# Three products of split weights as two, evictions in two halves, and output projections begun beside the last attention heads

## The reference

```python
def swiglu(h, w1, w3, w2):
    return (jax.nn.silu(h @ w1) * (h @ w3)) @ w2

def retention_layer(x, g, w_in, w_mem_kv, w_out, mem_n):
    h = rmsnorm_2(x, g)
    q, k, v, gate_r, mq, gate_m = split_cols(h @ w_in, [...])
    q = rotary(q...); k = rotary(k...) * (RET_DK ** -0.5)
    o = retention(q, k, v)
    o = o * lax.rsqrt(jnp.mean(o * o, axis=-1, keepdims=True) + EPS)
    o_ret = o * jax.nn.silu(gate_r)
    o_mem = memory_branch(mq, gate_m, mem_n, w_mem_kv)
    return x + jnp.concatenate([o_ret, o_mem], axis=-1) @ w_out

def dilated_layer(x, g, w_in, w_mem_kv, w_out, mem_n, kv):
    parts = split_cols(rmsnorm_2(x, g) @ w_in, ...)
    outs, lses = [], []
    for gi, (window, dil) in enumerate(DIL_CONFIG):          # three groups, 16 heads
        o, lse = dilated_group(q, kv[2 * gi], kv[2 * gi + 1], dil, window // dil)
    alpha = jax.nn.softmax(jnp.stack(lses, axis=0), axis=0)
    o = jnp.sum(alpha[..., None] * jnp.stack(outs, axis=0), axis=0)
    o_dil = o * jax.nn.silu(gate_d)
    return x + jnp.concatenate([o_dil, o_mem], axis=-1) @ w_out
```

## Time and profile before

| | us |
|---|---|
| median of 3 runs (lowest, highest) | 4314.84 (4308.7, 4323.8) |
| profiled execution, its own time | 4317.47 |
| its span, first to last instruction | 4315.7 |
| PE busy | 4001.4 (93%) |
| ACT, DVE, POOL busy | 1566.1, 1525.2, 1355.2 |
| mean granted clock of PE | 0.967 of full |

### The profile page before, as it was taken

How to read it: one execution, slowest core, us unless ns; L and a number is a source line. 1 busy time by engine, 2 the same in 40 slices (tenths; PEclk the granted TensorE clock), 3 DMA queues, 4 the chain that set the end, 5 groups by cost and what they waited for, 6 DMA issues and landing times.

```text
span 4315.7 us, 95444 instructions
## 1 busy us (share of the span) xinstructions
PE 4001.4 (93%) x42564; PEld 3762.1 (87%) x42564; DVE 1525.2 (35%) x2011; ACT 1566.1 (36%) x1954; POOL 1355.2 (31%) x632
## 2 busy tenths in 40 slices
PE   8999999899888999999989999898999999999978
PEld 6876778788877899999989899788899999999978
DVE  2142116566555433332342333333222222222232
ACT  3342226421213443443434334344333333333333
POOL 2321122000003344444433344343333333333333
PEclk9999999899998999999989999899999999999989
DMA  9887663000004455555535444344545444455434
GB/s 320 280 294 261 222 238 119 26 4 4 4 10 148 154 186 182 182 186 183 182 124 164 149 153 162 126 155 148 174 151 164 159 152 146 152 162 161 150 124 132
DMA packets 183175, 668.39 MB, mean 155 GB/s; under 512 B 20432, under 2 KB 20432, under 8 KB 182384
## 3 DMA queue, kind: packets, MB, share of 16 engines
q1 hardware_dynamic: 176544, 642.07, 45.2%
q10 hardware_dynamic: 4944, 16.03, 1.1%
q0 software_dynamic: 1280, 4.20, 0.2%
HBM read 653.82 MB, written 8.39 MB: 153 GB/s over the span
## 4 chain that ended last, share of the span: by engine, by line
PE 84%; DVE 6%; ACT 3%; issue 3%; DMA 2%; POOL 1%; POOLq 0%; ACTq 0%; DVEq 0%; SPq 0%
PE ps L921 66%; PE ps L882 2%; PE ps L1138 2%; PE ps L1162 2%; PE ps L1152 1%; ACT wh L1389 1%; PE ps L1074 1%; DVE wl L1858 1%; PE ps L1377 1%; PE ps L1361 1%; DVE tm L1861 1%; ACT xw L1389 1%; DVE cols L2336 1%; PE ps L1263 1%; PE ps L861 1%
## 5 line engine op out<-in xcount | busy, mean ns | idle before, releaser
L921 PE MATMUL ps<-halves,wh 128*128 128x256 f32 (+1 forms) x13632 | 2620.2, 294 | 77.9 <-DVE halves L1858 19.7
L921 PEld LDWEIGHTS ps<-halves,wh 128*128 128x128 f32 x13632 | 2184.1, 195 | 147.1 <-issue 84.8
L921 PE MATMUL ps<-halves,wl 128*128 128x256 f32 (+1 forms) x6816 | 1983.3, 291 | 0.0
L2410 POOL TENSOR_TENSOR wl<-raw,wh 128x1024 fp32r<-128x1024 f32 x508 | 1235.4, 2433 | 2066.6 <-ACT wh L1389 2066.5
L1389 ACT ACTIVATE wh<-raw 128x1024 fp32r<-128x1024 f32 x1016 | 1072.1, 1057 | 1531.2 <-PE ps L921 1174.7
L1858 DVE TENSOR_TENSOR wl<-raw,wh 128x1024 fp32r<-128x1024 f32 x508 | 688.6, 1356 | 2037.4 <-ACT wh L1389 2037.4
L921 PEld LDWEIGHTS ps<-halves,wl 128*128 128x128 f32 x6816 | 1327.5, 195 | 13.2
L921 PE MATMUL ps<-wh,halves 128*128 128x256 f32 x2688 | 498.6, 285 | 0.0
L921 PEld LDWEIGHTS ps<-wh,halves 128*128 128x128 f32 x2688 | 423.5, 192 | 10.3 <-issue 9.1
L921 PE MATMUL ps<-wl,halves 128*128 128x256 f32 x1344 | 380.7, 283 | 0.0
L921 PEld LDWEIGHTS ps<-wl,halves 128*128 128x128 f32 x1344 | 258.4, 192 | 0.4
(11 more groups left out here) (243 smaller groups left out, 2505.6 us busy)
## 6 DMA issues: line engine op xcount, KB each, us to landing
raw<-in_ffn SPq DMA_DIRECT2D x264, 512.0 KB, 4.0
raw<-in_ada SPq DMA_DIRECT2D x192, 512.0 KB, 4.5
raw<-in_w_kv SPq DMA_DIRECT2D x192, 512.0 KB, 3.3
raw<-in_w_in_b SPq DMA_DIRECT2D x160, 512.0 KB, 3.9
raw<-in_w_in_a SPq DMA_DIRECT2D x128, 512.0 KB, 3.6
raw<-in_mem SPq DMA_DIRECT2D x64, 512.0 KB, 5.4
raw<-in_w_out_a SPq DMA_DIRECT2D x48, 512.0 KB, 4.1
raw<-in_w_out_b SPq DMA_DIRECT2D x48, 512.0 KB, 4.1
```

The costliest lines, as they stand in the source:

```text
L921: p = self.e.matmul(o, x, y, start=bi not in begun, stop=final and kc == 3 and m == 2, skip_group_check=True)
L2410: return self.e.tensor_tensor(out, a, b, op)
```

## The change

- `products` has two new kinds, "WB" and "WA". Of the three products of a slice and part, two become one with 512 columns: the high half of the weights meets high and low halves of the activations side by side (or the high half of the activations both halves of the weights). The 256-column product low by high is added into the first 256 columns. The two sums of high and low parts, in columns 0 to 255 and 256 to 511 of a bank, are added when they are taken out. So a job fills two banks of the four.
- Every such job is emptied in two operations: ACT copies the low columns, DVE adds the high ones (`low`, `high`, `finish_on`, `glu_gate`, `swiglu`, `ev_x` with four operations of DVE in place of two). The first five jobs' kind "both", `w_q`, `w_r`, `w_gd`, the first four jobs of `w_out`, and the first four of each output projection stay as they were.
- The rotation comes one tile later (`then_rotate`).
- Output projections: four jobs are begun with five of their six tiles beside the last heads (`EARLY`), and the tiles of the stream are ordered so.
- `pipeline_tight` puts 2, 3, 2, 4, 3 tiles between head steps in place of 2 each (`weave`).
- `wh` and `wl` become one buffer `whl`; the ring `w2` has ten places in place of eleven.

```diff
-    add("w_out_a", range(8), range(6))
+    def begun(name):
+        add(name, range(4), EARLY)
+        add(name, range(4), (3,))
+        add(name, range(4, 8), EARLY + (3,))
...
+def weave(g, steps, counts):
+    for n in itertools.cycle(counts):
+        rest(limited(g, n))
+        if next(steps, "end") == "end":
+            break
+    rest(g)
...
-                run_all((part(made[:7]), 2), (before, 1))
+                weave(part(made[:7]), before, (2, 3, 2, 4, 3))
...
+    def halved(self, kind, acts):
+        return [(i, 0, "WB", 128 * i, acts, 0) if kind == "B" else (i, 0, "WA", 0, acts, i) for i in range(2)]
...
-                if kind == "B":
+                if kind[0] == "W":
+                    o = self.G(job.banks[bi]).rearrange("p (a n) -> p a n", a=2)
+                    if kind == "WB":
+                        wh, wl = hi[:, kc, c0:c0 + 128], lo[:, kc, c0:c0 + 128]
+                        pairs = [(o[:, 0], wl, ah), (o, wh, self.hl[acts][:, :, k, :])]
+                    else:
+                        r = slice(128 * tb, 128 * tb + 128)
+                        both = self.A("whl")[:, :, t.n % NW, 256 * kc:256 * kc + 256]
+                        pairs = [(o[:, 0], al[:, r], hi[:, kc, :]), (o, ah[:, r], both)]
...
+    def then_rotate(self, g):
+        for _ in g:
+            if self.turns:
+                self.rotate(*self.turns.pop())
+            yield
...
-    def project(self, name, which, r):
-        f = self.fence()
-        self.wait_at_project = f
-        for k in range(6):
-            c = 4 * k
-            self.split_mix((name, k), "HA" if k < 4 else "HB", c % 16, 4, c)
+    def project(self, name, which, r, heads, beside):
         outs = [(0, 256 * fb, "B", 128 * fb, "wide", 0) for fb in range(2)]
-        for n in range(8):
-            rest(self.gemm(name, n, range(6), outs, "v", lambda j, n=n: self.ev_x(j, n, None, r)))
+        jobs = [self.gemm(name, n, EARLY + (3,), outs if n < 4 else self.halved("B", "wide"), "v" if n < 4 else "v2",
+                          lambda j, n=n: self.ev_x(j, n, None, r)) for n in range(8)]
+        self.used_before = dict(self.used)
+        mixed = (self.mix_done(name, k) for k in EARLY)
+        for _ in range(2):
+            next(mixed)
+        run_all((heads, 1), (mixed, 2), (chain(*[limited(g, 5) for g in jobs[:4]]), beside))
+        self.f9 = self.fence()
+        if which:
+            self.reload_x2()
+        self.mix_done(name, 3)
+        for g in jobs:
+            rest(g)
...
+    def glu_gate(self, job, j):                      # DVE
+        s = self.work4[j % 4]
+        th, v = s[:, 0:2, :], s[:, 2:4, :]
+        self.wait_ge("glu_s", (j, "a"))
+        self.tt(v, v, self.high(job), ADD).then_inc(self.sig("ev_v", (job.key, 0)), 1)
...
     def swiglu(self, job, j, pos):                   # DVE
...
+        self.wait_ge("glu_s", (j, "b"))
+        self.tt(b, b, self.high(job), ADD).then_inc(self.sig("ev_v", (job.key, 0)), 1)
+        self.wait_ge("ev_v", (job.key, 0))
+        self.wait_ge("glu_v", (j, "a"))
+        self.stt(v, v, 0.5, b, MUL, MUL).then_inc(self.sig("glu_v", (j, "ab")), 1)
...
-        if kind == "plain":
+        if kind[:3] != "rot":                        # ACT
             self.ring_free(m)
-            self.act(dst, b.rearrange("p (c n) -> p c n", c=2), ACT.Copy).then_inc(self.sig("ev_s", (job.key, 0)), 1)
+            self.act(dst, self.low(job), ACT.Copy).then_inc(self.sig("ev_s", (job.key, "low")), 1)
+            if kind == "gated":
+                self.wait_ge("ev_v", (job.key, 0))
+                self.act(dst, self.gate_sum, ACT.Tanh, scale=0.5).then_inc(self.sig("ev_s", (job.key, "th")), 1)
```

More of the change, by code:

```diff
@@ L93, in weight_stream @@
         add("w_in_b", [24 + p])
-    add("w_out_b", range(8), range(6))
+    begun("w_out_b")
     out, n, a = [], 0, 0
@@ L2519 @@
 SHIFTED = (1, 2, 3)
+ROT_SCALE = {"rot_q": 1.0, "rot_k": 128 ** -0.5}
 COLS = {}
```

205 lines of the change are left out of this document (120 added, 85 removed).

## The result

| kernel | median of runs (lowest to highest) | profiled span |
|---|---|---|
| before | 4313.5 us (4308.7 to 4323.8, 4 runs) | 4315.7 |
| changed | 4207.2 us (4205.0 to 4210.0, 4 runs) | 4203.1 |

A forecast was written before the change was run, and what follows sets the result against it. PE's stream of weight products bounds the kernel (PE 84% of the chain of waits). Terms -91 + 3.4 + 3 - 16 - 19 - 14 = -134 take 4317.5 to 4184, 4181 as a median; range 4130 to 4210.

The forecast's parts named there:

- Two products in place of three: All 872 tiles of new kinds: 0.107 us saved a tile, 93 us, less 2 given back at the memory tiles.
- wrong: the period of 2.77 missed: Sign against the forecast: ACT's high halves in the feed-forward stage not starting every 2.77 us.
- Back-to-back issue gap: Skill's 131 ns a product of 512 columns would bring some 760 us; the prediction kept the measured 0.2267 us.
- Evictions: End of each job: the added copy and addition are covered by three tiles, 7.5 us against 8.3, cost 0.
- The norms' term: Jobs followed by a norm: four DVE additions in the open in place of two, +3.4 us.
- Rotation: Rotation a tile later: waits of 1.6 and 2.9 us, 18 in all against 14.6 before, so +3.
- Dilated heads: Seven groups beside tiles: waits 7.4 us a group, 1.6 gained, plus 0.7 of clock, -16 us in all.
- Parity: Dilated transposes: after odd numbers of tiles the last low half is POOL's, taking DVE's 1.23 us off the chain.
- the rival of an unheld scaling: Dilated softmax: POOL does not hold DVE's scaling up, 52 us gained in place of 16, 4145 us; chance 27%.
- The projections: Both output projections: early tiles fill the last heads' waits, -19 us at the first and -14 at the second.
- The sum: Whole kernel: all terms together -134 us, 4317.5 to 4184 profiled, 4181 as a median.

The follow-up runs named there:

- e1: The changed kernel with two tiles between all steps of the dilated heads, as before the change: 4251.4 us, ratio 0.9857.
- e7: The changed kernel with each rotation straight behind its job, as before the change, in place of a tile later: 4203.2 us, one run.
- e6: The changed kernel with both rotations of a retention job in the two halves of one bank: 4171.8 us, ratio 0.9681.
- e2: The changed kernel with three tiles ahead of the dilated heads' first step and two between all others: 4195.3 us, ratio 0.9732.
- e3: The changed kernel with the scaling of the dilated softmax on ACT in place of DVE: 4176.0 us, ratio 0.9692.
- e11: The changed kernel with one small extra product at one place, ahead of ffn3 in pair 12 of the feed-forward stage: 4211.1 us, one run.
- e4: The changed kernel with a small extra product ahead of ffn3 at pairs 0, 8 and 16 of the feed-forward stage: 4203.6 us, ratio 0.9747.
- e9: The changed kernel plus the edits of e3, e6 and e4, other dilated tile counts, one tile before the last dilated heads, memory maxima first: 4101.1 us, ratio 0.9500.
- e10: The kernel of e4 run once more, for its feed-forward stage: 4193.4 us, one run.

## Why the prediction was right, and where its size was off

The forecast was -134 us between profiled executions; -112.6 was measured. The step that was mis-sized most is the first term.

**Two products in place of three.** The mechanism holds, and at the high clock the size too where the spacing is 346.7 ns: there a tile takes 2.773 us. In the feed-forward stage the forecast was 27.4 us. Executions at 346.7 ns a pair gain 27.1 (755.0 in e1 and e7 against 782.1), the profiled one of the changed kernel 14.2. The term of 93 us took it that the earlier trace rows, with wide products one after the other, and the earlier trace rows, with narrow ones, carry over to a stream that alternates. They do not always: here the step failed, by 13 us in the execution that was compared. The bounds "0 to 93" held it, the value chosen was its upper end. By the prediction's own sign ("wrong: the period of 2.77 missed") the profile shows 2.83, not by waits of PE but by PE itself.

A second part of the same term is small and was missed as well. At 1.2 GHz a narrow product takes 0.213 us and a wide one 0.427, just twice it, so that a pair takes 0.640, as three narrow ones did. A cold tile gains nothing. In the changed kernel 5.9 tiles of `w_in_a` and 4.1 of the first `w_in_b` run so: about 1 us.

**Back-to-back issue gap.** The Trainium skill ("TensorE: Matmul & The Clock Gate", Back-to-back issue gap) gives 131 ns for a product of 512 columns in a stream with its loads. The traces do not agree: at the high clock the next product starts 0.227 to 0.241 us after a wide one, and the measurement decides, as it did ahead.

**Evictions.** Cost 0 was right in mid-stage. PE's idle time in the feed-forward stage is 10.2 us, 9.6 before, and no row has PE waiting for a bank there. The norms' term was forecast at 3.4 us and L1315 waits 8.7 us against 5.8: 2.9.

**Rotation.** 18 us forecast, 17.6 us in the stage, one wait a pair for the sine as named. In the order of the queue (`rot_q`, `rot_k`) the waits were 2.7 and 2.1 in three groups of heads and 1.1 and 2.2 in the first, where 2.9 and 1.6 were named. e7 and e6 show the mechanism.

**Dilated heads.** The waits are 1.68, 1.47, 1.27 and 1.89, 6.3 us a group in place of 7.4, so 2.7 us gained and not 1.6. Each wait is 0.2 to 0.3 us under its term: the sum let the whole of the scaling run behind POOL's end, and it ended its own time less 0.20 us behind it. Parity (e2) and POOL's hold on the scaling (e3) are shown; the rival of an unheld scaling, given 27%, is out: it took 1.33, 1.79, 1.91 and 0.81 us. The last is nearly free, though it stands behind a job's end: POOL's low half ran from 3314.84 to 3317.20 there, and the scaling began at 3316.82. The forecast had it held as well. The rule of the Trainium skill ("SBUF — State Buffer", Who interferes with whom) says that two-port modes of DVE are locked out for the whole of a GpSimd instruction. The trace agrees: begun beside POOL, the scaling ended 0.22 us (384 columns) or 0.42 us (768) after POOL had. From group to group the gain is 136.30 - 129.57 = 6.7 us where 4.3 + 1.6 + 0.7 = 6.6 was the sum. That the two agree is partly luck: the waits gave 1.1 us more than their term, and PE's busy time 4.0 where products and clock were to give 5.0. The stage's -54.0 is luck too, by the 5 us that most profiles of this program take more.

**The stages with memory heads.** Their waits are not in the forecast. `w_in_a` gained 4.8 us in place of 10.7. PE is busy 11.0 us less there, and not the 13.7 of 128 tiles: 0.6 of the difference are cold tiles, the rest is open. And it is idle 6.2 more: 3.0 at the rotation, as forecast, 1.9 at the memory heads' transposes (10.8 to 12.7), 0.8 ahead of the norm's sums. The first tiles of `w_in_b` gained 2.8 us of PE and idled 2.8 more (POOL's low half 9.7 to 11.2, the norm 0.7, the transposes 0.3, ACT's high half 0.3). A tile that is 0.107 us shorter also covers 0.107 us less at each wait that stands behind tiles, and the prediction counted that for the dilated groups alone. That is argued from the trace; no run separates it. Some 3 us a stage of the gain were never there to be had.

**The projections.** a: waits of 3.7 and 2.0 where 3.6 and 1.9 were named, and the stage gained 20.3 us of 20.7. b: 3.9, 10.8 for four waits and 4.1, where 3.7, 9.0 and 3.8 were, and 11.6 us of 15.7: 2.3 too little for waits. The prediction's 12 us for head products at full clock have no row; the rule that it used for a gives 20.14 x 0.69 = 13.9, and by this estimate 1.9 us of the gain were counted too much.

**The sum.** -134 against -112.6 between the profiles: 13.2 in the feed-forward stage, 5.9 in `w_in_a`, 4.7 in `w_in_b`, 4.1 in projection b, 2.4 in the memory stage, 0.4 in projection a, against 5.1 more in the dilated stage, 3.7 in RWKV and 0.5 in `w_out`. The 5.1 and the 3.7 are within what those stages vary by from execution to execution.

## What to carry to other kernels

When a stall stands behind a pipeline of tiles that two engines finish in turn, don't count the tiles between; ask which engine's piece is last, and what else that engine's piece holds up. When PE's pieces get shorter, take their lost cover at every wait off the gain, and look for a clock that falls behind waits that grew. A bank that two steps share in turn may be the wait: taking it away brought 25 us (e6), where moving the step a tile on had brought under 1. And the prices of two instructions, each in a stream of its own kind, made up the fastest spacing seen in a stream that alternates (0.120 + 0.2267 us), and most starts of the long stream missed it: take such a sum as the upper end of a gain, and compare spacing, not busy time.

## What the runs showed of the hardware

- A stream of alternating products of 256 and 512 columns runs in one of several rhythms, 346.7 or 353.3 ns a pair, and keeps it over 1938 pairs. One small product in between changed 353.3 to 346.7 (e11), and nine stretches behind such a product, in e4, e9 and e10, were all at 346.7. Behind the products of heads and norms 572 streams were fast and 18 slow. Without a product in between the same stage had 353.3 in six of nine starts.
- At 1.2 GHz a product of 512 columns took as long as two of 256 (0.427 and 0.213); at 2.4 GHz 0.227 and 0.120, 13 ns less than two.
- Waits of 1.80 and 2.72 us at the transposes went with a clock of 0.99 over the group (before), waits of 1.90 and 2.82 with 0.96 (e1): PE was busy 3.3 us longer in e1's group than in the changed kernel's, for the same products.
- The same program fell to the lower clock five, six or seven times in its dilated stage, in different executions, and took 982.0 to 987.5 us for it.
- DVE's scaling, SBUF to SBUF, took 1.91 us for 384 columns beside POOL (0.42 alone) and ended 0.22 us after POOL's instruction.
- ACT's copy with a scale for each partition, 384 columns in SBUF, took 0.62 us beside POOL's instruction, and 0.61 without it.
